# SiLU's activation table set loaded ahead of the experts' loop of a two-layer decoder step

## The reference, cut to what matters

```python
def _swiglu(x, w_gu, w_down):
    g, u = jnp.split(x @ w_gu, 2, axis=-1)
    return (jax.nn.silu(g) * u) @ w_down

def _moe(x, w_router, w_exp_gu, w_exp_down):
    logits = (x @ w_router).astype(jnp.float32)
    top_v, top_i = lax.top_k(logits, TOP_K)
    gates = jax.nn.softmax(top_v, axis=-1)
    gate = jnp.sum(jax.nn.one_hot(top_i, N_EXPERTS, dtype=jnp.float32) * gates[..., None], axis=-2)
    out = jnp.zeros_like(x)
    for e in range(N_EXPERTS):
        out = out + _swiglu(x, w_exp_gu[e], w_exp_down[e]) * gate[..., e:e + 1].astype(x.dtype)
    return out
```

## Time and profile before

| what | us |
|---|---|
| median of 3 runs | 1769.95 |
| lowest and highest run | 1766.35, 1770.01 |
| profiled execution | 1765.79 |
| its span (first to last instruction) | 1764.0 |
| TensorE's mean granted clock in it | 0.985 of full |

### The profile page before, as it was taken

How to read it: one execution, slowest core, us unless ns; L and a number is a source line. 1 busy time by engine, 2 the same in 40 slices (tenths; PEclk the granted TensorE clock), 3 DMA queues, 4 the chain that set the end, 5 groups by cost and what they waited for, 6 DMA issues and landing times.

```text
span 1764.0 us, 22681 instructions
## 1 busy us (share of the span) xinstructions
PE 1696.8 (96%) x8446; PEld 1319.4 (75%) x8446; DVE 1183.1 (67%) x1522; ACT 824.0 (47%) x853; POOL 142.8 (8%) x138
## 2 busy tenths in 40 slices
PE   7999999999999999999999999999999999999993
PEld 4645487689999664648767888888888888888883
DVE  2687535354543367663524798988888888888895
ACT  1122211144442212221112677777777778777772
POOL 0530000000000063000003200000000000000000
PEclk9999999999999999999998999999999999999997
DMA  9656553855534535655385689999999999999992
GB/s 319 199 204 215 214 197 109 294 186 175 179 132 144 181 122 204 217 218 191 139 302 182 213 301 366 394 361 390 364 388 375 376 378 376 387 373 382 373 397 64
DMA packets 220720, 466.71 MB, mean 265 GB/s; under 512 B 11150, under 2 KB 50248, under 8 KB 220630
## 3 DMA queue, kind: packets, MB, share of 16 engines
q1 hardware_dynamic: 213446, 444.76, 69.6%
q0 software_dynamic: 4896, 16.77, 3.4%
q10 hardware_dynamic: 2304, 4.20, 0.6%
HBM read 447.10 MB, written 18.74 MB: 264 GB/s over the span
## 4 chain that ended last, share of the span: by engine, by line
PE 85%; DVE 7%; ACT 3%; issue 2%; DMA 2%; SPq 1%; ACTq 0%; DVEq 0%; POOLq 0%
PE bank L1227 83%; PE bank L1231 3%; DVE arena L2674 1%; DVE ring_low L2154 1%; ACT high L1778 1%; DMA out<-mem_rows 1%; DVE R L2288 0%; DMA y_rows<-arena,slot_row 0%; ACT arena L1842 0%; DVE st L2646 0%; DVE st L2567 0%; ACT SQ L1863 0%; SPq L730 0%; SPq L736 0%; DVE pair_in L2307 0%
## 5 line engine op out<-in xcount | busy, mean ns | idle before, releaser
L2154 DVE TENSOR_TENSOR ring_low<-ring,high 128x2048 fp32r<-128x2048 f32 x264 | 600.7, 2291 | 88.6 <-ACT high L1778 87.6
L1778 ACT ACTIVATE high<-ring 128x2048 fp32r<-128x2048 f32 x264 | 505.5, 1919 | 136.6 <-PE bank L1227 127.6
L1227 PE MATMUL bank<-high,xg_high 128*128 128x512 f32 x704 | 278.9, 396 | 4.4 <-DVE ring_low L2154 4.4
L1227 PE MATMUL bank<-ring_low,xg_high 128*128 128x512 f32 x704 | 275.1, 391 | 0.0
L1227 PE MATMUL bank<-high,xg_low 128*128 128x512 f32 x704 | 275.0, 391 | 0.0
L1227 PEld LDWEIGHTS bank<-high,xg_high 128*128 128x128 f32 x704 | 132.6, 188 | 34.9 <-DVE ring_low L2154 8.5
L1227 PEld LDWEIGHTS bank<-ring_low,xg_high 128*128 128x128 f32 x704 | 132.6, 188 | 28.3
L1227 PEld LDWEIGHTS bank<-high,xg_low 128*128 128x128 f32 x704 | 132.7, 189 | 26.3
L1842 ACT ACTIVATE arena<-bank 128x512 f32<-128x512 f32 (+3 forms) x89 | 43.1, 521 | 210.9 <-PE bank L1227 141.4
L1227 PE MATMUL bank<-high,he_high 128*128 128x512 f32 x352 | 139.1, 395 | 0.0
L1227 PE MATMUL bank<-ring_low,he_high 128*128 128x512 f32 x352 | 137.2, 390 | 0.0
(11 more groups left out here) (321 smaller groups left out, 2424.3 us busy)
## 6 DMA issues: line engine op xcount, KB each, us to landing
ring<-in_w_exp_gu SPq DMA_DIRECT2D x176, 1024.0 KB, 13.8
ring<-in_w_exp_down SPq DMA_DIRECT2D x40, 2048.0 KB, 15.8
ring<-in_w_in SPq DMA_DIRECT2D x12, 2048.0 KB, 11.6
ring<-in_w_ffn_gu SPq DMA_DIRECT2D x22, 1024.0 KB, 8.6
ring<-in_w_ckv SPq DMA_DIRECT2D x8, 2048.0 KB, 8.2
ring<-in_cache_mem_k SPq DMA_DIRECT2D x16, 1024.0 KB, 8.2
ring<-in_cache_mem_v SPq DMA_DIRECT2D x16, 1024.0 KB, 6.8
ring<-in_cache_attn_k SPq DMA_DIRECT2D x32, 256.0 KB, 4.2
```

Of the source, the lines that this page charges most:

```text
L1227: return M.matmul(out, lhsT, rhs, start=start, stop=stop)
L1778: S.activation(high_bufs[h % HIGH_BUFS][:], ring[:, s, j * HALF:(j + 1) * HALF], ACT.Copy).then_inc(split_high, 1)
L2154: V.tensor_tensor(ring_low[:, s, part], ring[:, s, part], high_bufs[h % HIGH_BUFS][:], ALU.subtract).then_inc(split_low, 1)
```

## The change

One instruction is asked for on ACT, ahead of the waits that stand before the experts' loop:

```diff
@@ -65,6 +65,7 @@
 HALF = SLOT // 2
 assert EPOS % RING == 0 and HALVES % HIGH_BUFS == 0
 EXP_AND_LN = "natural_log_exp_and_others"
+SILU = "silu_and_others"
 LAM_INIT = [0.8 - 0.6 * math.exp(-0.3 * l) for l in range(L)]
 
 
@@ -1816,6 +1817,7 @@
                     expert(e, c)
 
 
+            S.preload_act_table_set(SILU)
             xT_dve.wait(act, L - 1, 1)
             act.wait_ge(pos_known, 1)
             act.wait_ge(y_rows_written, rows_written(0, 0))
```

## The result

| | before | after |
|---|---|---|
| median (6 runs each), us | 1768.61 | 1757.17 |
| lowest and highest, us | 1766.35, 1770.01 | 1756.83, 1760.77 |
| profiled execution, us | 1765.79 | 1756.83 |
| its span, us | 1764.0 | 1755.0 |

The ratio is 0.9943, with a 95% interval of 0.9928 to 0.9958: the kernel is faster, by 7 to 13 us. The forecast was 1763.7 us in a range of 1758.8 to 1767.5.

The account below looks back on a forecast made before the run. PE, busy 96% of the span, was taken as the bound, pausing about 0.9 us at seven expert heads behind ACT's load. Gains of 6.1 + 0 + 0 + 0, said as 6.2, from 1769.95 gave 1763.7 us, range 1758.8 to 1767.5.

Parts of the forecast that it names:

- The path: At an expert's head, ACT's table load delays h2 on ACT, then `ring_low` on DVE, and this stops PE.
- Part 1: Removing the load ahead of h2 gains 0.90 us at expert 1, 0.86 at six others, 6.1 us in all.
- The eighth load ahead of h2: The load at expert 0, where PE starts at half clock; removing it was put at nothing.
- Part 2: Removing the load ahead of SiLU, eight times: worth nothing by itself, but without it the pause would return at h4.
- Part 3: One load added ahead of the loop, before the wait for `y_rows_written`: cost 0; without that cover 1.28 us once.
- The weights: The loop's weight stream can keep up with turns 0.9 us shorter; a tight chunk's 3.5 us reserve falls to 2.6.
- The sum: 6.1 us from the load ahead of h2, nothing elsewhere, 6.2 with the small wait at h4.
- (a): Another wait, DVE's loop turn or ACT's register work, replaces most of the pause; 2.1 to 4.2 us left; chance 0.10.
- (b): The whole load at the head lies on the path: 7 x 1.29 = 9.0 us, 1760.9 us; chance 0.03.
- (c): The weights' stream becomes the loop's bound, from the fifth turn nothing gained: about 3.5 us, 1766.4; chance 0.03.
- (d): The loop's loads stay or move within the body, or something unseen hides the gain: 1770 us; chance 0.04.
- (e): Without pauses PE's granted clock falls to half once per expert in the loop: 10 us slower, 1780; chance 0.03.

Follow-up runs that it names:

- one load at the head: SiLU's set loaded once per expert at the head of the loop's body, ahead of h2, nothing ahead of the loop; 1768.59 us, ratio 1.0002 to the kernel before.
- that run: The changed kernel with one load per expert put back between the split of h3 and the first SiLU; 1764.49 us, ratio 0.9959 to the kernel before.
- the larger comparison: Both kernels measured again unchanged: 34 runs of the kernel before, median 1768.68 us, 11 of the changed kernel, 1761.58 us; ratio 0.9957.
- after again: The changed kernel, unchanged, measured a second time beside the kernel before; 1761.58 us (11 runs), ratio 0.9957.
- two loads at the head: The changed kernel with two loads per expert (Exp's set, then SiLU's) at the head of the loop's body; 1777.69 us, ratio 1.0051 to the kernel before.

## Why the prediction was right and where it was wrong

**The path** (load, h2 on ACT, `ring_low` on DVE, PE) was right: with the load ahead of h2 back, the pause is back; with only the other one back, it isn't.

**Part 1**, 0.90 us at expert 1 and 0.86 at the others, 6.1 in all. Measured by the one load at the head: 94.24 to 93.34, 0.90 each, 6.3 us in the loop. The term was 0.2 us too small. It kept 0.04 to 0.06 us of each pause as a remainder, because it counted the 0.34 us behind a matmul that had to wait, also for a matmul that comes on time; in after the starts are 0.23 and 0.24 apart, and the remainder is about 0.01. That DVE's turn costs nothing, as PE's does, was right.

**The eighth load ahead of h2**, that of expert 0, was put at nothing, rightly: with it back (one load at the head), expert 0 is as long as in after (95.03 and 95.01 us). What expert 0 lost, it lost to the load at SiLU. The timeline of PE in before, at its h4, shows a small pause:

```profile
993.84 0.39 PE L1227 MATMUL bank<-ring_low,xg_high 128*128 128x512 f32 x1
994.10 0.50 PE L1227 MATMUL bank<-high,xg_high 128*128 128x512 f32 x1
994.44 0.40 PE L1227 MATMUL bank<-high,xg_low 128*128 128x512 f32 x1
```

From 993.84 to 994.44 it is 0.60 us in place of 0.45, most of the 0.2 us that expert 0 gained. The prediction had nothing for it: it looked for PE's waits only at the seven turns.

**Part 2**, nothing by itself, with 0.1 us in the sum for the small wait at h4: it was 0.5 us, 0.2 at expert 0 and some 0.04 at each other. That the pause would return at h4 in full was wrong by a factor of five (0.17 us), for the reason given at that run.

**Part 3**: right, and covered twice.

**The weights**: right. In after the stream still dips, to 227 GB/s from 1337 to 1338 us and to 129 from 1354 to 1355, and the tight chunk of the head, issued at 1357.1 and 1357.6, keeps 2.6 us as foretold: its later load landed 17.7 us on, at 1375.3, and ACT used it at 1377.94.

```profile
DMA to landing us min/median/max: 15.6/16.6/17.7
...
1377.94 1.92 ACT L1779 ACTIVATE high<-ring 128x2048 fp32r<-128x2048 f32 x1 [0.80 <-PE bank L1228]
```

**The sum**, 6.2 us, against 6.8 us in the loop: 0.2 short in part 1 and 0.4 in part 2. The mechanism was right and the sizes nearly so.

**The step that failed** is the one from the sum to the time. The prediction took its width from the baseline of four executions, 1765.8 to 1770.0 us, and set the lower end by the lowest of them. It had then no room for the six runs of after being low ones. By 34 runs before varies over 11.5 us. Of the 6.5 us between forecast and time, 1.3 are the base (1769.95 from three runs, 1768.61 from six), 0.6 the sum, and 4.6 lie outside the loop. By the larger comparison (1768.68 to 1761.58 us, 7.1) and the loop (6.8 to 7.3) the forecast's difference of 6.2 was 0.6 to 1 us short; the first comparison showed 11.4, and the 4.6 us beyond the loop's are of the stretches that differ by 5 to 8 us between two executions of the same kernel. The second comparison doesn't show them again, so I call them spread. The granted clock supports this: two of the six runs of after had 0.986, two 0.985 and two 0.984, while no run of before whose clock is on record has more than 0.985 and the median of its 34 is 0.984; and at 0.984 the two took 1759.8 and 1760.8 us, within the 1759.8 to 1762.4 of after again at that clock. Why those six runs had so high a clock isn't shown.

**The rivals.** (a) no wait took the place: PE was busy for all 743 us from 985 to 1728 us; (b) the second load at the head shows that 1.26 us would be lost if DVE were free, so the cover by line 2191 is what kept the first at 0.9; (c) didn't happen, the period is 93.34 or 93.35 us at every turn, nor did (d). (e) the clock was 1.00 from 985 to 1728 us in after, without any pause; where it did fall once, in the kernel with two loads at the head, it was behind a longer pause, the opposite of what (e) feared.

## What to carry to other kernels

An operation on an engine that is less than half busy costs what is left of it after the nearest cover, and this is read at one place: the idle time of the engine behind it (DVE, 0.82 us) and what that engine does just before (line 2191), not the operation's own length. The same load cost 0, 0.17, 0.9 or 1.26 us per expert by where it stood. A state that a loop's body leaves as it needs it can be set once ahead of the loop; and if it must be set inside, the place ahead of a wait was free here (1.23 us of idle time for a load of 1.28, with 0.4 us to spare behind it). Size the range of a forecast of half a percent by the spread of the whole program, and judge the change by the part of the trace that hardly varies: here the loop, stable to half a microsecond while the rest moved by eight.

## What was unexpected of the hardware

- A load of a table set took 1283 ns in all 215 cases in the ten traces, also where the set was already there, and nothing more: an operation with nothing else to wait for, be it a load, starts 1.29 to 1.30 us after the load's start.
- The program's time outside the loop varies by 8 us between executions of the same kernel (1009.0 to 1016.9 us in before). 3 us of this are the same 96 small matmuls at a different granted clock. Over 34 runs of before, each 0.001 less of mean granted clock goes with about 2 us more of time.
- After one pause (2.27 us from start to start) of seven alike, PE's granted clock fell to the lower level for about eight matmuls, which cost 1.6 us; after the other six it didn't. The one with the drop was the first turn of the loop; what set it apart isn't shown.
